# Compressed attention as pairs of units in main attention's sequence, float32 probabilities copied once, values unsplit

## The reference, cut to what matters

```
def masked_softmax(s, mask):
    s = jnp.where(mask, s, NEG)
    m = jnp.max(s, axis=-1, keepdims=True)
    p = jnp.where(mask, jnp.exp(s - m), 0.0)
    return p / jnp.maximum(jnp.sum(p, axis=-1, keepdims=True), TINY)
# compressed branch: 63 keys, one per 16 tokens
s_c = jnp.einsum('bqghd,bngd->bghqn', q, kc) * SCALE + rb[rel_bucket(dist_c)]
o_c = jnp.einsum('bghqn,bngd->bqghd', masked_softmax(s_c, dist_c >= 0), vc)
# selected branch (here all keys of the prompt, causal) and window branch (512 keys)
o = gates[:, :, 0][..., None] * o_c + gates[:, :, 1][..., None] * o_s + gates[:, :, 2][..., None] * o_w
# FoX: causal attention over all 1024 keys with a bias from cumulated log-forget values
```

## Time and profile before

| | before |
|---|---|
| median of 3 runs | 2075.52 us |
| profiled execution, its time | 2079.37 us |
| its span | 2077.6 us |
| PE busy | 1869.2 us (90%) |
| DVE busy | 1011.2 us (49%) |
| ACT busy | 735.0 us (35%) |
| compressed attention | from 684.2 us |
| main attention | 747.9 to about 1157 us |

### The profile page before, as it was taken

How to read it: one execution, slowest core, us unless ns; L and a number is a source line. 1 busy time by engine, 2 the same in 40 slices (tenths; PEclk the granted TensorE clock), 3 DMA queues, 4 the chain that set the end, 5 groups by cost and what they waited for, 6 DMA issues and landing times. The chain is left out here.

```text
span 2077.6 us, 31665 instructions
## 1 busy us (share of the span) xinstructions
PE 1869.2 (90%) x11624; PEld 1633.9 (79%) x11624; DVE 1011.2 (49%) x1899; ACT 735.0 (35%) x1456; POOL 543.1 (26%) x626
## 2 busy tenths in 40 slices
PE   2998999998867889988989798999999999799995
PEld 2887877997644777777777586999999999776674
DVE  2323521333333557777777653323332333366997
ACT  2233411212212157777777532111211211133352
POOL 4310022422362422222211201111221122143452
PEclk9899999999988579999999899999999999999998
DMA  6453353356996943332211122111111111064533
GB/s 146 89 116 110 121 164 120 108 187 201 312 248 215 226 132 69 68 66 62 62 47 62 64 82 74 40 49 40 45 56 40 40 50 61 18 227 142 184 137 133
DMA packets 168966, 229.21 MB, mean 110 GB/s; under 512 B 44717, under 2 KB 113126, under 8 KB 168712
## 3 DMA queue, kind: packets, MB, share of 16 engines
q1 hardware_dynamic: 144282, 154.58, 24.8%
q0 software_dynamic: 24560, 73.03, 12.8%
HBM read 192.59 MB, written 40.18 MB: 112 GB/s over the span
## 5 line engine op out<-in xcount | busy, mean ns | idle before, releaser
L121 PE MATMUL gate_acc<-o_T_hi,w_gate_split_hi 128*128 128x352 f32 x528 | 171.1, 324 | 2.3 <-ACTq L2696 2.3
L2322 DVE TENSOR_TENSOR pa_probs_T_lo<-pa_t,pa_probs_T_hi 128x512 fp32r<-128x512 f32 (+3 forms) x288 | 148.1, 533 | 49.7 <-ACT pa_probs_T_hi L2253 45.4
L121 PE MATMUL up_acc<-o_T_hi,w_up_split_hi 128*128 128x352 f32 x528 | 171.0, 324 | 0.7 <-DVEq L2739 0.7
L122 PE MATMUL up_acc<-o_T_lo,w_up_split_hi 128*128 128x352 f32 x528 | 169.9, 322 | 0.0
L122 PE MATMUL gate_acc<-o_T_lo,w_gate_split_hi 128*128 128x352 f32 x528 | 169.9, 322 | 0.0
L123 PE MATMUL up_acc<-o_T_hi,w_up_split_lo 128*128 128x352 f32 x528 | 169.8, 322 | 0.0
L123 PE MATMUL gate_acc<-o_T_hi,w_gate_split_lo 128*128 128x352 f32 x528 | 169.6, 321 | 0.0
L2253 ACT ACTIVATE pa_probs_T_hi<-pa_t 128x512 fp32r<-128x512 f32 (+3 forms) x288 | 132.3, 473 | 80.2 <-PE pa_t L2177 74.3
L2177 PE MATMUL pa_t<-ident,pa_scores 128*128 128x128 f32 x816 | 138.4, 275 | 19.2 <-DVE pa_probs_T_lo L2322 18.2
L2238 ACT ACTIVATE pa_scores<-pa_scores,pa_neg_max 128x128 f32<-128x128 f32 (+1 forms) x192 | 143.5, 747 | 27.3 <-DVE pa_neg_max L2276 23.6
L121 PE MATMUL y_acc<-w_down_split_hi,act_split_hi 128*128 128x512 f32 x308 | 125.1, 406 | 20.0 <-DVE act_split_lo L3061 19.2
(11 more groups left out here) (441 smaller groups left out, 4776.2 us busy)
## 6 DMA issues: line engine op xcount, KB each, us to landing
w_down_raw<-in_w_down SPq DMA_DIRECT2D x59, 512.0 KB, 4.5
fox_k_pages<-in_cache_fox_kv SPq DMA_DIRECT2D x64, 256.0 KB, 7.1
w_rows<-in_cache_fox_kv POOLq DMA_DIRECT2D x48, 256.0 KB, 8.5
w_gate<-in_w_gu SPq DMA_DIRECT2D x22, 512.0 KB, 3.8
w_up<-in_w_gu SPq DMA_DIRECT2D x22, 512.0 KB, 3.7
w_rows<-in_w_in SPq DMA_DIRECT2D x5, 2048.0 KB, 9.3
sel_pages<-in_cache_nsa_kv POOLq DMA_DIRECT2D x64, 128.0 KB, 7.9
pa_k_fox<-scratch_kf_d POOLq DMA_DIRECT2D x32, 256.0 KB, 6.3
```

Source lines behind the costliest of these rows:

```text
L121: pe.matmul(out, a[0][at], b[0][bt], start=start, stop=False)
L122: pe.matmul(out, a[0][at], b[1][bt], start=False, stop=False)
L2322: dve.tensor_tensor(lo, PT[n % 2][:, 0:m * P].rearrange("p (m n) -> p m n", n=P), hi, ALU.subtract).then_inc(s_cd, 1)
```

## The change

The compressed stage is dissolved. Each of its 8 tiles is now a pair of units of 4 heads (one for each key group) and runs through main attention's steps and buffers. Four of these pairs stand ahead of main attention's first pair, and one each follows the first four main pairs. Its scores of a unit are now four matmuls on the same 64 rows. The exponentiated scores' sums are taken on DVE, per unit, and the coefficients by pair.

In main attention the probabilities stay float32 and are copied once: ACT copies the even chunks and DVE the odd ones. The value tile is one plain float32 tile of 64 columns, loaded straight into place, and nothing splits it. `values` is one block behind the first unit's turns. It has one float32 product per key tile. These go by turns to partitions 0 to 63 and 64 to 127 of `pa_o`, and the halves are added after `back`, as before.

The core of the diff:

```diff
-        self.v = {kind: [ph.sb(f"pa_v_{kind}{u}", [P, NT, 2, HD], FR) for u in range(2)] for kind in kinds}
+        self.v = {kind: [ph.sb(f"pa_v_{kind}{u}", [P, NT, HD]) for u in range(2)] for kind in kinds}
-    def split_values(self, pool, dst, raw, sem, at):
-def compressed_attention(c, pa):
...
-    units = [(i, j, t) for i in range(NH) for j in range(NJ) for t in range(NT)]
+    main = [[(i, j, t), (i, j, t + 1)] for i in range(NH) for j in range(NJ) for t in range(0, NT, 2)]
+    cmps = [[(g, CMP, t) for g in range(G)] for t in range(NT)]
+    pairs = cmps[:4]
+    for n, pair in enumerate(main):
+        pairs = pairs + [pair] + cmps[n + 4:n + 5]
+    units = [unit for pair in pairs for unit in pair]
...
-        pT = [split(ph, f"pa_probs_T{i}", [P, NT + 1, 2, P]) for i in range(2)]
+        pT = [ph.sb(f"pa_probs_T{i}", [P, NT + 1, 2, P]) for i in range(2)]
...
+            def compressed_scores(s):
+                g, _, t = units[s]
+                if s == 0:
+                    pe.wait_ge(c.s_cq, 16 * G)
+                pe.wait_ge(s_m, max(0, s - 1) + 1)
+                rows = slice(g * HD, (g + 1) * HD)
+                for m in range(GH):
+                    ins = pe.matmul(S[s % 2][:, m * NC:(m + 1) * NC], c.ca_q[rows, m, t * P:(t + 1) * P], c.kc_p[rows, :],
+                                    start=True, stop=True)
+                ins.then_inc(s_s, 1)
...
                 if n >= 2:
-                    pe.wait_ge(s_cd, n - 1)
+                    pe.wait_ge((s_ca, s_cd)[n % 2], n // 2)
...
+            def values(p):
+                last = of_unit[2 * p + 1][-1]
+                pe.wait_ge(s_ca, last // 2 + 1)
+                pe.wait_ge(s_cd, (last + 1) // 2)
+                if cmp(2 * p):
...
+                pe.wait_ge(s_n, max(1, p))
+                for y, (slot, key) in enumerate(mine):
+                    side = y % 2 * HD
+                    ins = pe.matmul(O[p % 2][side:side + HD, 0:2 * P], v[kind][u][:, key, :],
+                                    pT[p % 2][:, slot, :, :].rearrange("p a n -> p (a n)"), start=y < 2, stop=y >= n - 2)
...
             for s in range(0, NU + 8, 2):
-                now = [of_unit[e] if 0 <= e < NU else [] for e in (s - 2, s - 1)]
-                rounds = max(1, len(now[0]) + len(now[1]))
                 p = (s - 4) // 2
                 for side in range(2):
                     if s + side < NU:
                         scores(s + side)
+                    if side == 1 and 0 <= (s - 6) // 2 < NPR and not cmp(s - 6):
                         back((s - 6) // 2)
...
-                            values(p, x / rounds, (x + 1) / rounds)
+                    if side == 0 and 0 <= p < NPR:
+                        values(p)
...
+            def compressed_max(s):
+                g, _, t = units[s]
+                x = heads(sc[s % 3][:, 0:GH * NC])
...
+                chain(dve.tensor_tensor(x, heads(S[s % 2][:, 0:GH * NC]), c.cb[:, g * GH:(g + 1) * GH, 56 - 8 * t:56 - 8 * t + NC], ALU.add))
+                chain(dve.tensor_reduce(cmx[:, :], x, AX, ALU.max))
...
+                        if n % 2 == 1:
...
+                            dve.tensor_copy(pT[e // 2 % 2][0:rows, slot:slot + m, e % 2, :],
+                                            PT[1][0:rows, 0:m * P].rearrange("p (m n) -> p m n", n=P)).then_inc(s_cd, 1)
...
-                compressed_attention(c, pa)
                 prompt_attention(c, pa)
```

More of the change, by code:

```diff
@@ L1983, in prompt_attention, with cmp, main_pairs, column @@
     NJ = len(jobs)
-    units = [(i, j, t) for i in range(NH) for j in range(NJ) for t in range(NT)]
-    NU = len(units)
+    CMP = NJ
     PJ = NT // 2
     NK = 2 * NJ * NT
+    main = [[(i, j, t), (i, j, t + 1)] for i in range(NH) for j in range(NJ) for t in range(0, NT, 2)]
[4 more added lines that the diff above has]
+    units = [unit for pair in pairs for unit in pair]
+    NU, NPR = len(units), len(pairs)
+    at_unit = {unit: s for s, unit in enumerate(units)}
+    def cmp(s):
+        return units[s][1] == CMP
+    def main_pairs(p):
+        return sum(1 for x in range(max(0, p)) if not cmp(2 * x))
+    def column(s):
+        i, j, t = units[s]
+        return ((i * NJ + j) * NT + t) % NK
     def first_tile(s):
         i, j, t = units[s]
-        return max(0, t - WIN // P) if jobs[j][1] == "win" else 0
+        return max(0, t - WIN // P) if j < CMP and jobs[j][1] == "win" else 0
     def tiles(s):
-        return units[s][2] + 1 - first_tile(s)
-    NPR = NU // 2
+        return GH if cmp(s) else units[s][2] + 1 - first_tile(s)
     def slots(s):
@@ L2178, in turn @@
                 ins.then_inc(s_t, 1)
-            def values(p, begin, end):
+            def values(p):
[4 more added lines that the diff above has]
+                    pe.wait_ge(s_n, max(1, p))
+                    for h in range(H):
+                        g, m = h // GH, h % GH
+                        ins = pe.matmul(O[p % 2][:, h * HD:(h + 1) * HD], pT[p % 2][0:NC, 1 + m, g, :],
+                                        c.vc_p[:, g * HD:(g + 1) * HD], start=True, stop=True)
+                        if m == GH - 1:
+                            ins.then_inc(s_o, 1)
+                    return
                 i, j, t = units[2 * p]
@@ L2219, in _ @@
                         scores(s + side)
-                    if side == 1 and 0 <= (s - 6) // 2 < NPR:
+                    if side == 1 and 0 <= (s - 6) // 2 < NPR and not cmp(s - 6):
                         back((s - 6) // 2)
-                    for n in now[side]:
-                        turn(n)
-                        if live:
-                            values(p, x / rounds, (x + 1) / rounds)
-                        x += 1
-                if live and not x:
-                    values(p, 0, 1)
+                    if 0 <= s - 2 + side < NU:
+                        for n in of_unit[s - 2 + side]:
+                            turn(n)
+                    if side == 0 and 0 <= p < NPR:
+                        values(p)
         @block.scalar
@@ L2292, in output @@
                     cj = co[:, j * NT:(j + 1) * NT]
[L2293 removed]
+                    ins = dve.reciprocal(cj, sm[:, column(s) + 1 - NT:column(s) + 1])
                     if kind != "fox":
```

318 lines of the change are left out of this document (115 added, 203 removed).

## The result

The changed kernel takes 2093.05 us (median of 6 runs, 2086.95 to 2095.34) against 2076.99 us for the one before in the same session (6 runs, 2072.51 to 2080.76): ratio 1.0076, 95% interval 1.0056 to 1.0096. The forecast was 2033.5 us and faster. The kernel became some 16 us slower, and the time lies outside the range.

A forecast was written before the change was run, and what follows sets the result against it. PE was taken to bound both stages, with DVE's serial chain behind ACT making its gaps. Main attention -44 us (gaps -39, values -5) and head +2 gave -42 on 2079.4 us: 2037.4, 2033.5 as a median; range 2000 to 2066.

The forecast's parts named there:

- Column time of the values: Main attention's values: 928 float32 records at 0.105 us, halves side by side, 98 us in place of 111.
- No overlap: Rival, chance 0.09: value column halves don't run side by side, 0.213 us a record, about 2115 us.
- Gaps: PE's gaps in main attention: 3.1 to 1.4 us a job over 23 jobs, 39 us less, through DVE's and ACT's saved copy work.
- Change of form: Entering and leaving the half-width form at 96 value blocks: 15 us, of which 7 hidden in waits.
- 0.10 on entry, 0.06 lost: Loss in us around a value block, read from an earlier stage's eight column-half records of 192 columns.
- Head: Compressed pairs and first four main pairs: 78 us in place of 75.8, +2 us, bounds -11 and +18.
- the forecast's cut: Boundary between head and main attention at the first selected scores, 760.0 us in the earlier trace.
- 27 us alone: Head's first part: four compressed pairs ahead of main attention, at the low clock, 27 us.
- 48 us of alternation: Head's second part: main and compressed pairs by turns, 48 us, between 35 (DVE-bound) and 64 (low clock).
- the clock rival: Rival, chance 0.12: the clock stays low until the compressed pairs are through, 64 instead of 48 us, 2050 us.
- 0.20 us more a block: Upper bound of the values' term in main attention: dearer form changes make it +10 instead of -5 us.
- 0.65 us a job with -13: Lower bound of main attention's part, -66 us: smallest gaps, and value products without change cost.

The follow-up runs named there:

- e7: Kernel before with its value products in one block behind the first unit's turns, two copies kept: 2112.74 us, ratio 1.0157 to the kernel before.
- e1: Changed kernel with the compressed stage kept apart, new copies and column-half values kept: 2074.88 us, ratio 0.9992 to the kernel before.
- e10: e1 with the values late, behind the second unit's scores and `back`, ahead of its turns: 2059.6 us, ratio 0.9902 to the kernel before.
- e4: Changed kernel with the value block moved behind the second unit's scores and `back`, ahead of its turns: 2053.32 us, ratio 0.9885 to the kernel before.
- e12: Changed kernel with the compressed stage kept and values dealt out behind each turn, 192 pieces for 96 blocks: 2091.77 us, ratio 1.0066 to the kernel before.
- e2: Changed kernel with full-width value products, leaving out one of two key tiles' probabilities (output incomplete): 2067.2 us, ratio 0.9945 to the kernel before.
- e6: e4 with full-width value products, leaving out one of two key tiles' probabilities (output incomplete): 2029.05 us, ratio 0.9759 to the kernel before.
- e9: e4 with compressed units of two heads of each group, score products taking row halves by turns: 2041.99 us, ratio 0.9825 to the kernel before.

## Why the prediction was wrong

**Column time of the values: right.** 0.105 us a record was forecast, 0.103 to 0.108 was measured, which gives 12 us. No overlap, the slow rival, did not come. What the forecast drew from the Trainium skill (TensorE: Matmul & The Clock Gate, What overlaps and what doesn't), that column halves on the same rows would gain nothing, is not what the trace has: two records of such halves start 0.007 us apart.

**Gaps: the step that failed.** The forecast let PE's gaps fall by 39 us, from 3.1 to 1.4 us a job. The 1.4 came out. For 23 jobs it is 32 us, and the changed kernel's PE is idle for 34.1 us of the 399 from the first selected scores on, with 28.3 us in the three rows above. The 3.1 was wrong. It is the stage's time less a count of PE's work, 71 us for 23 jobs, and the forecast took all of it for waits that a shorter chain would end, because 31.0 + 22.3 + 18.2 us of the earlier trace rows come to about as much. But the 31.0 us are idle time of PEld, the weight loads, on the same 47 occasions on which PE waits the 22.3 us for `output`; they overlap and were counted twice. The earlier trace rows would have shown it: in 397 us PE is busy for 353.3, so it was idle for 43.7, and 34.1 were left of that. Gaps fell by 10 us in place of 39. The other 27 us or so of the old gaps were no waits, and they stayed; what they consist of is open.

**What the move did inside this.** The waits fell little for a reason that the forecast didn't price by itself. The same edit moves the values from behind every turn into one block. e7 shows the move alone at +33 us for the old copies, with 29 us more of turns' waits; at that place the new copies and halves are worth the 34 us (e1 against e7), and the two cancel. With the values late 17 us (stage kept, e10) to 24 us (e4) against the kernel before are kept. Keeping the old order would not: e12 shows that pieces behind every turn pay the change of form twice as often.

**Change of form: mis-sized.** "0.10 on entry, 0.06 lost" came from one place where a 24-record block of nearly the same form followed, so it showed no real way out. Into 128-column work the exit costs 0.15 to 0.3. Charged were 8 us for 96 blocks (15, less 7 hidden); e2 and e6 measured 27 and 26 by medians, 21 and 23 in the traces. That is 12 to 19 us of the miss. The rule from the Trainium skill (TensorEngine Tiling, Key Properties) that a change of mode drains TensorE agrees in kind; it gives no size.

**Head: +2 forecast, +12 measured** by the forecast's cut, inside the bounds of -11 and +18. Its parts were 27 us alone (26.1 measured), then 48 us of alternation: from the first FoX scores to the first selected ones, behind which only the last compressed pair's turns and values stand, the trace has 59. The forecast charged nothing for compressed values that wait for DVE's output of the compressed pair before, and asked the clock rival only about how long the low level lasts. Late values bring the head, cut as in the table, to 88.3, row halves by turns to 76.7.

**Together.** In the two stages the forecast had -42 us and the two traces have +10.8, a miss of 53: gaps 29, change of form 12 to 19, head 10. The table's rest closes too: column time -12, waits -11, change of form +20 (e2) make -3, and -3.1 is measured. The other 7 us of the 60 between 2033.5 and 2093.05 lie outside these stages (2.3) and in how the two profiled executions stand to their medians. By medians the steps are: place +33 (e7), copies and halves -34 (e1), stage dissolved +17, together +16; this sum closes by construction.

Two bounds of the forecast don't follow from its own numbers: 0.20 us more a block gives +14 and not +10, and 0.65 us a job with -13 gives -69 and not -66. Nothing hangs on either.

What stays open: why the first 0.1 and the last 0.15 to 0.3 us of a block are lost. The profile shows the next weight load idle with nothing that it waits for, and no run changed that alone.

## What to carry to other kernels

Before a gap is promised away, compare it with the engine's own idle time in the windows, and don't add the waits of weight loads to those of the matmuls that follow them. When an edit makes a chain shorter and moves work in the same stroke, price the move by itself: what filled the waits at the old place, and what does the moved block wait for at the new one. Take the cost of a form from a place with the same neighbours on both sides, not from its inside. And if a change loses a little though its parts look good, try the block one slot later before undoing it: here one moved call was worth 40 us.

## What the hardware did unexpectedly

- Half-width float32 products side by side among full-width work cost 0.23 to 0.37 us a block in the timelines, 0.27 by medians and 0.22 to 0.24 by the traces of two stages (e2, e6), as much as two or three of the records themselves.
- Two column halves whose records are neighbours in the queue run side by side: 0.107 us a record of 256 columns, against 0.213 for a full-width one in e6.
- At the lower clock, 64-row products whose neighbours alternate between the row halves are 0.10 us apart, on the same half 0.22 (e9 and the changed kernel above, 1.12 and 1.96 us for eight).
